# Expert rows added to the residual in DRAM by the scatter, in place of a weighted combine at the end

## What is computed

```
xt = RMSNorm(x)                                  # 520 rows of 1024
p_top, g = top1(softmax(xt @ wg + bg))           # one of 4 expert groups
top_l, e = top2(logits of group g)               # two of its 8 experts
w  = softmax(top_l) * p_top                      # two weights per token
h  = silu(xt @ w1[e]) * (xt @ w3[e])             # per expert: 1024 -> 256
y  = sum over the two experts of  w * (h @ w2[e])
x  = x + y
out = RMSNorm(x) * final_g
```

## Time and profile before

| what | value |
|---|---|
| median of 3 runs | 661.05 us (660.33 to 662.53) |
| span of the profiled execution, first to last instruction | 656.5 us |
| time of its own for the profiled execution | not listed; the median lies 4.55 us over its span |
| PE busy | 510.5 us, 78% of the span |
| DVE, ACT, POOL busy | 230.2, 142.6, 79.2 us |
| bytes moved by DMA | 144.62 MB |

### The profile page before, as it was taken

How to read it: one execution, slowest core, us unless ns; L and a number is a source line. 1 busy time by engine, 2 the same in 40 slices (tenths; PEclk the granted TensorE clock), 3 DMA queues, 4 the chain that set the end, 5 groups by cost and what they waited for, 6 DMA issues and landing times. The chain is left out here.

```text
span 656.5 us, 6560 instructions
## 1 busy us (share of the span) xinstructions
PE 510.5 (78%) x2320; PEld 296.6 (45%) x2320; DVE 230.2 (35%) x519; ACT 142.6 (22%) x267; POOL 79.2 (12%) x129
## 2 busy tenths in 40 slices
PE   3999999999999989999459839395684929478800
PEld 3788888358888733545333313132231313123200
DVE  3353112694987565233721111111020111101158
ACT  7211044704256352212100000000010000001123
POOL 4000000100211211000030111102011111101014
PEclk9899999999999979999559869788795969779955
DMA  9403110412341439210969999999999999969263
GB/s 300 151 0 129 57 72 12 152 53 77 100 165 64 144 122 308 116 44 22 342 230 331 375 376 337 388 336 394 336 369 376 355 379 331 398 198 381 82 280 130
DMA packets 90494, 144.62 MB, mean 220 GB/s; under 512 B 6489, under 2 KB 72197, under 8 KB 85856
## 3 DMA queue, kind: packets, MB, share of 16 engines
q1 hardware_dynamic: 79608, 100.57, 45.9%
q10 hardware_dynamic: 3888, 28.31, 10.6%
q0 software_dynamic: 6976, 15.44, 7.1%
HBM read 137.49 MB, written 15.10 MB: 232 GB/s over the span
## 5 line engine op out<-in xcount | busy, mean ns | idle before, releaser
L1390 PE MATMUL ps<-XNT,WC 128*128 128x260 f32 x640 | 144.8, 386 | 1.2 <-PE ps L1390 0.6
L1390 PEld LDWEIGHTS ps<-XNT,WC 128*128 128x128 f32 x640 | 121.9, 192 | 23.3 <-issue 4.0
L1629 PE MATMUL ps<-WC,XRC 128*64 128x512 f32 x128 | 69.0, 700 | 66.7 <-DMA GY<-in_exp_w 66.7
L1294 DVE TENSOR_TENSOR XRC<-ps,XRC 128x256 f32<-128x256 f32 x16 | 6.8, 424 | 184.2 <-ACT XRC L810 184.2
L1629 PE MATMUL ps<-GY,XRC 128*64 128x512 f32 x128 | 69.0, 701 | 0.0
L1629 PEld LDWEIGHTS ps<-WC,XRC 128*64 128x64 f32 x128 | 19.8, 162 | 107.7 <-issue 107.6
L1629 PE MATMUL ps<-SLOT,XRC 128*64 128x512 f32 x240 | 59.0, 617 | 2.4 <-DMA SLOT<-in_exp_w 2.4
L1551 PE MATMUL ps<-WC,GY 128*128 128x512 f32 x128 | 58.6, 611 | 1.0 <-DVE GY L1184 0.6
L810 ACT ACTIVATE XRC<-ps 128x256 f32<-128x256 f32 x16 | 6.1, 383 | 209.2 <-PE ps L1629 209.2
L609 POOL DMA_INDIRECT expert_rows<-T,SIDX x16 | 16.1, 1008 | 236.9 <-ACT T L824 220.1
L1551 PEld LDWEIGHTS ps<-WC,GY 128*128 128x128 f32 x128 | 24.4, 196 | 29.4 <-issue 28.2
(11 more groups left out here) (273 smaller groups left out, 587.7 us busy)
## 6 DMA issues: line engine op xcount, KB each, us to landing
SLOT<-in_exp_w SPq DMA_DIRECT2D x32, 1024.0 KB, 12.4
WC<-in_exp_w SPq DMA_DIRECT2D x18, 1024.0 KB, 13.3
GY<-in_exp_w SPq DMA_DIRECT2D x16, 1024.0 KB, 17.7
WC<-in_exp_w ACTq DMA_DIRECT2D x14, 1024.0 KB, 8.5
SLOT<-in_exp_w ACTq DMA_DIRECT2D x13, 1024.0 KB, 8.8
WC<-in_w_in SPq DMA_DIRECT2D x6, 2048.0 KB, 9.2
WC<-in_w_out SPq DMA_DIRECT2D x2, 2048.0 KB, 7.8
X<-in_x_prompt SPq DMA_DIRECT2D x4, 512.0 KB, 4.7
```

What stands on the lines that cost most here:

```text
L1294: dve.tensor_tensor(HG[p], PS[2 + p][:, FE:2 * FE], HS[p], ALU.mult).then_inc(s_hg, 1)
L1390: ins = pe.matmul(ps[:, 0:HALF], WC[:, j % 2, k, m * P:(m + 1) * P], XNT[:, k, hf * HALF:(hf + 1) * HALF], start=(k == 0), stop=(k == KD - 1))
L1629: ins = pe.matmul(PS[2 + p][at:at + CAP, :], XGT[p][:, k, at:at + CAP], weights[two][0][:, k, :], start=(k == 0), stop=(k == KD - 1), tile ...
```

## The change

- Before the experts, SP also stores the residual rows `X` to `xr_dram` (`residual_rows`, 520 rows), tile by tile, and POOL waits for these five stores before the experts start.
- The ten comparisons become one operation of DVE over 640 columns, into a buffer of its own, and the table's matmuls (now `slot_table`) start when all of it is there.
- The gate weights are computed in front of the expert stage, put into one-hots (`OHW`), and a second `slot_table` of the same size makes the weight of every slot, `WSL`. PE does it between the first and the second `turn`. `gated` multiplies by that weight.
- The scatter adds (`compute_op=ALU.add`) to `xr_dram`, by `SRCI`, and each scatter first waits until the scatter before it has landed.
- The pair q is now experts q and q + 16 (`expert(e)`), which lie in different groups, so no token is twice in one scatter.
- At the end SP reads five tiles of sums straight into `X`; the combine on DVE is gone, and POOL and ACT no longer take part in the final scaling.

```diff
+                sp.wait_ge(s_opr, 2 * i + 2)
+                sp.dma_start(xr_dram[c * P:c * P + ROWS[c], :], X[0:ROWS[c], c, :]).then_inc(s_xrow, 16)
                 sp.wait_ge(s_xs, NT + i + 1)
...
+        def expert(e):
+            return e // 2 + NPAIR * (e % 2)
...
-                sp.dma_start(YE[c][0:ROWS[c]], ye_v[c * P:c * P + ROWS[c]]).then_inc(s_ye[c], 16)
+                sp.dma_start(X[0:ROWS[c], c, :], xr_dram[c * P:c * P + ROWS[c], :]).then_inc(s_ye[c], 16)
...
+            pool.wait_ge(s_xrow, 16 * NT)
...
                 pool.wait_ge(s_yd, n + 2)
+                pool.wait_ge(s_ys[1 - p], 16 * use + 16 * p + 16)
                 pool.sem_inc(s_turn, 1)
-                pool.indirect_dma_start(out=ye_dram, out_offset=bass.IndirectOffsetOnAxis(ap=SIDX[:, p, :].bitcast(U32), axis=0),
-                                        in_=YO[p], in_offset=None,
-                                        bounds_check=2 * TOK - 1, oob_is_err=False).then_inc(s_ys[p], 16)
+                pool.indirect_dma_start(out=xr_dram, out_offset=bass.IndirectOffsetOnAxis(ap=SIDX[:, p, :].bitcast(U32), axis=0),
+                                        in_=YO[p], in_offset=None, bounds_check=TOK - 1, oob_is_err=False,
+                                        compute_op=ALU.add).then_inc(s_ys[p], 16)
...
-                dve.tensor_tensor(HG[p], PS[2 + p][:, FE:2 * FE], HS[p], ALU.mult).then_inc(s_hg, 1)
+                dve.scalar_tensor_tensor(out=HG[p], in0=PS[2 + p][:, FE:2 * FE], scalar=w, in1=HS[p],
+                                         op0=ALU.mult, op1=ALU.mult).then_inc(s_hg, 1)
...
-                    dve.tensor_scalar(PM[:, j % NPM, :], iota_s, RANK[:, k, i:i + 1], None, ALU.is_equal).then_inc(s_pm, 1)
+                dve.tensor_tensor(PM, bc(iota_s, 1, 2 * NT), bc(RANK[:, :, :].rearrange("p k i -> p (k i)"), 2, CAP),
+                                  ALU.is_equal).then_inc(s_pm, 1)
...
                 turn(base, 0, half_n)
+                pe.wait_ge(s_wt, r + 1)
+                slot_table(OHW, NPAIR).then_inc(s_wtab, 1)
...
                 turn(base + 1, 1, half_n)
```

More of the change, by code:

```diff
@@ L456, in _ @@
             for e in range(2, 4):
-                load_w13(e, e)
-                load_w2(sp, e, e)
+                load_w13(expert(e), e)
+                load_w2(sp, expert(e), e)
             await_read(sp, ("lg", NT - 1))
@@ L478, in _ @@
                         sp.wait_ge(s_hw, r * NE + i * 4 + slot + 1)
-                        load_w13(i * 4 + slot + 4, slot)
+                        load_w13(i * 2 + expert(slot + 4), slot)
                 for slot in range(4):
@@ L603, in scatter @@
                 pool.sem_inc(s_turn, 1)
-                pool.tensor_copy(SIDX[:, p, :], DSTI[:, q]).then_inc(s_si, 1)
+                pool.tensor_copy(SIDX[:, p, :], SRCI[:, q]).then_inc(s_si, 1)
                 pool.wait_ge(s_si, n + 1)
@@ L821, in y_copy @@
                         if slot != KEPT % 4 or not last:
-                            load_w2(act, load + slot, slot)
+                            load_w2(act, load + expert(slot), slot)
                 act.wait_ge(s_ys[p], 16 * scattered + 16)
@@ L838, in two_pairs @@
                         silu(q, p)
-                        y_copy(q - 1, 1 - p, r * (NPAIR // 2) + i, load=i * 4 + 4, last=last)
+                        y_copy(q - 1, 1 - p, r * (NPAIR // 2) + i, load=i * 2 + 2, last=last)
                         ht_copy(q, p)
@@ L1307, in _ @@
                 dve.wait_ge(s_rdone, r + 1)
[L1308 to L1311 removed]
+                dve.wait_ge(s_pmu, r + 1)
+                dve.tensor_tensor(PM, bc(iota_s, 1, 2 * NT), bc(RANK[:, :, :].rearrange("p k i -> p (k i)"), 2, CAP),
+                                  ALU.is_equal).then_inc(s_pm, 1)
                 dve.wait_ge(s_tab, r + 1)
@@ L1334, in _ @@
[L1334 to L1339, removed]
-            dve.wait_ge(s_fg, 16)
[L1343 to L1360, removed]
@@ L1363, in _ @@
+            dve.wait_ge(s_fg, 16)
+            for c in range(NT):
+                n = ROWS[c]
+                dve.wait_ge(s_froot, c + 1)
+                dve.reciprocal(RSTD[0:n, c:c + 1], RSTD[0:n, c:c + 1]).then_inc(s_frstd, 1)
+                dve.wait_ge(s_frstd, c + 1)
+                dve.scalar_tensor_tensor(out=OUT[c][0:n], in0=X[0:n, c, :], scalar=RSTD[0:n, c:c + 1],
+                                         in1=FGB[0:n], op0=ALU.mult, op1=ALU.mult).then_inc(s_fin[c], 1)
         @block.tensor
@@ L1657, in down, with slot_table @@
                                 ins.then_inc(s_yw, 1)
+            def slot_table(rows, at_col):
+                for k in range(2):
+                    for i in range(NT):
+                        n = ROWS[TILE_ORDER[i]]
+                        for two in range(2):
+                            at = two * CAP
+                            ins = pe.matmul(PS[B_O][at:at + CAP, at_col:at_col + NPAIR], PM[0:n, NT * k + i, :],
+                                            rows[0:n, k, i, two * NPAIR:(two + 1) * NPAIR], start=(k == 0 and i == 0),
+                                            stop=(k == 1 and i == NT - 1), tile_position=(0, at), skip_group_check=True)
+                return ins
             pe.sem_inc(s_pmu, 1)
@@ L1662, in _ @@
                 base = r * NPAIR
[L1663 to L1677, removed]
+                pe.wait_ge(s_pm, r + 1)
+                slot_table(OHV, 0).then_inc(s_tab, 1)
                 half_n = r * (NPAIR // 2)
                 turn(base, 0, half_n)
+                pe.wait_ge(s_wt, r + 1)
+                slot_table(OHW, NPAIR).then_inc(s_wtab, 1)
+                pe.wait_ge(s_wtab, r + 1)
+                pe.sem_inc(s_pmu, 1)
                 turn(base + 1, 1, half_n)
```

68 lines of the change are left out of this document (40 added, 28 removed).

## The result

The change makes the kernel slower: 667.79 us median of 5 runs (665.09 to 668.82) against 661.47 (660.33 to 662.66) for the kernel before beside it, a ratio of 1.0099 with a 95% interval of 1.0073 to 1.0125, or +6.3 us. The forecast was 659.4 us in a range of 650.0 to 668.5. Of all runs one is left out, an execution of b7_nopool that took 2905 us.

What follows compares the result with a forecast made beforehand. The prediction took the DMA engines to pace the expert stage, with a serial end after it. End -12.3, head +1.5 and stage +9.1 us summed to -1.7 from 661.05, giving 659.4 us, range 650 to 668.5.

Steps and rivals of the forecast that it cites:

- the stage's term: Expert stage: each of 13 adding scatters costs one more DMA pass of 0.70 us, 9.1 us in all.
- is time the weights lose: Expert stage: scatters share the engines evenly with the weights, so their engine time, 9.1 us, lengthens the stage.
- are never free: Expert stage, 349.5 to 582 and 588 to 606 us: all 16 DMA engines always busy, shares 1.04 and 1.03.
- The head: Start of the expert stage: later first table and second table on PE delay the first `up` by 1.5 us.
- The work for the weights' one-hots: Before the first gathered rows: seven small operations, some 2 us, costed at nothing because the gather covers them.
- The end: After the last scatter's issue: shorter read-back and scaling gain 14.4 us, a later landing costs 2.1, net 12.3 us.
- the serial wait: Last scatters: scatter 16 waits for scatter 15 to land and issues at 624.7 instead of 623.86, 0.8 us later.
- The rival of serial landings: End: adds land at rest in 8.4 us, so scatter 16 lands 7.8 us later; 667.2 us, chance 0.08.
- the one with two more passes: Stage: each adding scatter costs 1.40 us more, so the stage grows 18.2 us; 668.5 us, chance 0.20.
- A hidden fetch: Stage: fetching old rows costs next to nothing beside other engine work; 650.2 us, chance 0.22.
- the distance from the first `up` to the last weights' arrival: Expert stage: growth under 4 us or over 15 would show the price of the add was wrong.
- sign for PE's waits on gathered rows: Expert stage: PE waiting for gathered rows would show POOL's new wait is on the path; no size given.

Runs made afterwards that it cites:

- b7_nopool: The kernel before, with DVE instead of POOL and ACT doing the final scaling of all five tiles; 659.16 us, ratio 0.9985.
- a1_plain: The changed kernel with a plain scatter in place of the adding one, sums left out of the result; 652.36 us, ratio to before 0.9864.
- b0_same: The kernel before, unchanged, run once more for a second profile; 659.77 us.
- a3: The changed kernel with an expert's rows dealt to even slots first, then odd ones; 661.99 us, ratio to before 1.0012.
- b3: The kernel before with an expert's rows dealt to even slots first, then odd ones; 660.70 us, ratio 0.9999.
- a4: The changed kernel with ten unused matmuls on PE ahead of odd pairs' `up`, except first and last; 663.74 us, ratio to before 1.0042.
- b4: The kernel before with ten unused matmuls on PE ahead of odd pairs' `up`, except first and last; 661.76 us, ratio 1.0008.
- a7_all: The changed kernel with the weights' table before the first `turn`, even slots first and ten unused matmuls before odd `up`s; 658.52 us, ratio to before 0.9974.
- a2_table_early: The changed kernel with the weights' table moved on PE ahead of the first `turn`; 665.86 us, ratio to before 1.0068.
- b5_add: The kernel before with its DRAM rows filled from the residual and the scatters adding, no serial wait or weight table; 674.82 us, ratio 1.0210.

## Why the prediction was wrong

The sign was wrong: -1.7 us forecast, +6.3 measured, and +8.0 between the two spans. The two sides of the sum were right, an end that gets shorter and a DMA-bound stage that pays for the add, but the sizes were not. Of the 9.7 us between -1.7 and +8.0 the stage has 6.0, the end 1.8, the head 1.1 and the part ahead of the changed code 0.7.

**The step that failed is the stage's term**, 9.1 us for 13 scatters, where the profile shows 15.1: 12.0 for the adds (a1_plain against the change) and 3.1 for the rest of the change, which the prediction put at nothing and whose cause stays open. The engine time was nearly right: 8.0 us for the 12 scatters up to 600 us. What failed is the sentence that the time a scatter takes "is time the weights lose", which makes the stage's loss equal to the mean engine time. That holds only while all engines stay full. The prediction read a mean share of 1.04 as engines that "are never free"; window by window b0_same has 4.8 us of dry time, and the change has 6.2 more. Two experiments take these apart:

- *Uneven load.* Spreading the filled slots gives 5.8 us back at the same bytes and engine time, and only where the scatter adds (a3 and b3). That the layout is the cause is shown. My explanation is that the DMA engines share a transfer by partition: with the rows in the first slots of each 64 some engines carry more of the add than others, and weights that all engines bring are complete only with the slowest. The views show only the mean of 16 engines, but the packet records bear out the first half, for a plain scatter at rest: the 80 rows of the last scatter form 16 chains, in each of which a packet starts as the one before ends, with 3 to 8 rows in b0_same and 4 to 6 in b3_spread. The second half is argued. Why plain scatters, loaded just as unevenly, cost no time by it (the sign that I had named against this explanation) stays open; their rows take 160 ns and not 327.
- *`up` at half clock.* Keeping PE at work gives 4.1 us back with the add and nothing without it (a4 and b4). Longer waits for weights end in longer `up`s (2.9 us in sum), these free their weight slots later, and the engines run dry behind them, as at 444 us. The prediction had no term for PE's clock; before the change the same waits cost nothing that b4_warm could give back.

The two overlap, by what a7_all gives back.

**The price of an add.** The engine time rose by 0.67 us a scatter, where the forecast had one more pass of 0.70; the time that the stage lost to the adds, 12.0 us, is more than that. The Trainium skill, page "Collectives: The Full Stack", section "The bandwidth ceiling: the fold count and why AG ≠ RS ≠ AR", says of the add in a ReduceScatter between ranks that it emits two reads for one write. The trace agrees in engine time also for a scatter inside one core (327 ns a row for 160). It shows a loss beyond that, on which the rule says nothing.

**The head**, +1.5 (0 to 1.8), came to 2.6. The first table starts 0.5 us later in its place (327.96 - 322.93 before, 329.22 - 323.66 after) and it is no quicker for having all comparisons done (2.79 us). From there to the first `up` it is 2.1 us more where I had allowed 1.2 at most; 1.65 of that lie between the two `turn`s, where the second table stands; a2_table_early gets 1.5 back. The work for the weights' one-hots was hidden, as forecast.

**The end**, -12.3, came to -10.5. Read-back and scaling were right: 14.4 us for 15.0. The scatter was not: an add lands in 5.56 us at rest, I took 4.5. And the serial wait cost 2.3 us instead of 0.8 (18.55 us from the last `up` to the last scatter's issue before, 20.82 now), since scatter 15 needs 6 us to land as well. Scatter 16 could have gone at 643.7, 0.85 us behind the last copy of its rows as in b0_same, and went at 645.98. The rival of serial landings had named this place, at 7.8 us.

**The rivals.** The time is nearest to the one with two more passes (668.5), but its mechanism did not occur: it named 1.40 us more of engine time a scatter, the runs show 0.67. That the range holds the measured time is luck, since its upper end was that rival's. A hidden fetch is ruled out by a1_plain and b5_add. Of the signs I had named, the distance from the first `up` to the last weights' arrival came out at the edge of "wrong" (+15), rightly. POOL's queue took half as much again (17.5 to 25.6 us), as said. The starts of the odd pairs' `up`s moved apart by 2.0 us per two pairs (36.3 to 38.4), where 1.4 was forecast for the ends of PE's waits before them. The sign for PE's waits on gathered rows shows too (13.8 us for 6.5 before), but POOL's new wait is not needed for most of it: b5_add has 11.0 us without that wait, and a1_plain 8.5 with it.

## What to carry to other kernels

In a stage paced by DMA, the mean engine time of added traffic is only a part of its price (8.0 of 12.0 us here); look also at the fullest engine and at what the consumer does with the longer wait, and ask whether the rows of an indirect transfer lie evenly over the partitions. Before moving work from a quiet end into such a stage, hold the end's gain against that price: here 10.5 us gained at the end, 15.1 paid in the stage. Small new work on a critical engine belongs into a wait that is already there, as the weights' table before the first `turn`; here that is 1.5 us in place, too little for the times to settle.

## What the runs showed of the hardware that was not expected

- An indirect scatter that adds holds POOL for 1.57 us instead of 0.97 to issue some 264 KB, and lands at rest in 5.56 us instead of 3.2.
- In one stretch with the same bytes on POOL's queue (gathers and scatters together), the adds raise the engine time from 2.6 to 3.8 us of 16 engines per MB (17.5 and 25.6 us for 6.73 MB). A 4 KB row that is added takes about 327 ns of an engine, one that is written about 160.
- The layout of the filled rows is worth 5.8 us of 667.8 with adding scatters and nothing with plain ones (660.70 for 661.13). In a plain scatter of 80 rows at rest the fullest of 16 chains of packets holds 8 rows packed and 6 spread.
- A higher mean granted clock (0.926 for 0.886) left the time of the kernel before as it was, within 0.3%.
